# Low parts of split weight chunks: one GpSimd subtraction over eight feature blocks, or four over two

## What is computed

```python
def ab_layer(x, xc, mod, mod_c, w_in, w_out, ...):
    q, k, v, g_a, xb, b_g, c_g, g_b = split_cols(modulate(x, shift, scale) @ w_in, widths)
    ...
    y = jnp.concatenate([o_a * jax.nn.silu(g_a), o_b * jax.nn.silu(g_b)], axis=-1) @ w_out
    x_new = layer_norm(DEEPNORM_ALPHA * x + gate * y, ln_g, ln_b)
    ...
def swiglu(x, w_gate, w_up, w_down):
    return (jax.nn.silu(x @ w_gate) * (x @ w_up)) @ w_down
```

## Time and profile before

| | us |
|---|---|
| median of three runs | 2348.47 |
| lowest, highest | 2347.04, 2351.69 |
| span of the profiled execution | 2345.2 |

### The profile page before, as it was taken

How to read it: one execution, slowest core, us unless ns; L and a number is a source line. 1 busy time by engine, 2 the same in 40 slices (tenths; PEclk the granted TensorE clock), 3 DMA queues, 4 the chain that set the end, 5 groups by cost and what they waited for, 6 DMA issues and landing times. The chain is left out here.

```text
span 2345.2 us, 28077 instructions
## 1 busy us (share of the span) xinstructions
PE 2188.8 (93%) x11735; PEld 1760.2 (75%) x11735; DVE 1079.0 (46%) x1662; ACT 669.4 (29%) x1035; POOL 786.9 (34%) x373
## 2 busy tenths in 40 slices
PE   4999888989999999998898899999998999999998
PEld 3887777866686767886855678888887688888886
DVE  1113664653656565657995543111126684111114
ACT  3223233324545454542112432100113353000111
POOL 1421113401322333325500015553544234554453
PEclk7999999999999999999899999999999999999999
DMA  9232113422111111113111112322322222232322
GB/s 301 70 116 77 55 55 113 123 90 90 36 36 37 36 36 37 36 55 99 41 36 54 55 55 72 103 95 91 108 90 90 82 98 72 90 108 90 94 95 81
DMA packets 174797, 187.47 MB, mean 80 GB/s; under 512 B 25600, under 2 KB 153936, under 8 KB 174544
## 3 DMA queue, kind: packets, MB, share of 16 engines
q1 hardware_dynamic: 164720, 175.42, 24.0%
q10 hardware_dynamic: 9376, 8.16, 1.2%
q0 software_dynamic: 576, 2.10, 0.2%
HBM read 183.56 MB, written 2.10 MB: 79 GB/s over the span
## 5 line engine op out<-in xcount | busy, mean ns | idle before, releaser
L3018 POOL TENSOR_TENSOR weights_lo<-weights_raw,weights_hi 128x2048 fp32r<-128x2048 f32 (+1 forms) x101 | 458.1, 4536 | 858.5 <-ACT weights_hi L1421 662.2
L698 PE MATMUL ring<-input_hi,weights_hi 128*128 128x512 f32 x784 | 305.4, 389 | 4.1 <-POOL weights_lo L3018 4.1
L700 PE MATMUL ring<-input_hi,weights_lo 128*128 128x512 f32 x784 | 305.1, 389 | 0.0
L699 PE MATMUL ring<-input_lo,weights_hi 128*128 128x512 f32 x784 | 305.0, 389 | 0.0
L2845 DVE CAST weights_hi<-weights_raw 128x2048 fp32r<-128x2048 f32 (+1 forms) x72 | 87.6, 1216 | 366.5 <-PE ring L700 174.3
L3006 POOL TENSOR_TENSOR h_w<-h_p 128x512 f32<-128x512 f32 x56 | 72.0, 1286 | 414.9 <-PE ring L1009 310.9
L982 PE MATMUL obank<-acts,weights_raw 128*128 128x512 f32 x384 | 178.5, 619 | 0.0
L698 PEld LDWEIGHTS ring<-input_hi,weights_hi 128*128 128x128 f32 x784 | 147.2, 188 | 36.2 <-issue 5.8
L700 PEld LDWEIGHTS ring<-input_hi,weights_lo 128*128 128x128 f32 x784 | 147.2, 188 | 30.6
L699 PEld LDWEIGHTS ring<-input_lo,weights_hi 128*128 128x128 f32 x784 | 147.2, 188 | 30.4
L991 PE MATMUL obank<-weights_raw,acts 128*128 128x256 f32 x640 | 143.2, 381 | 0.0
(11 more groups left out here) (464 smaller groups left out, 4394.4 us busy)
## 6 DMA issues: line engine op xcount, KB each, us to landing
weights_raw<-in_w_ada SPq DMA_DIRECT2D x24, 1024.0 KB, 5.3
weights_raw<-in_ffn_w_gate SPq DMA_DIRECT2D x22, 1024.0 KB, 5.4
weights_raw<-in_ffn_w_up SPq DMA_DIRECT2D x22, 1024.0 KB, 5.3
weights_raw<-in_w_in_c SPq DMA_DIRECT2D x20, 1024.0 KB, 5.1
weights_raw<-in_ffn_w_down SPq DMA_DIRECT2D x16, 1024.0 KB, 5.0
weights_raw<-in_w_in_ab SPq DMA_DIRECT2D x9, 1024.0 KB, 6.8
weights_raw<-in_ev_w_in SPq DMA_DIRECT2D x8, 1024.0 KB, 5.4
weights_raw<-in_od_w_in SPq DMA_DIRECT2D x8, 1024.0 KB, 5.3
```

The costliest lines, as they stand in the source:

```text
L698: pe.matmul(o, hi[:, k, ms], xh[:, k, t0:t0 + n], start=k == 0, stop=False)
L699: pe.matmul(o, hi[:, k, ms], xl[:, k, t0:t0 + n], start=False, stop=False)
L700: last = pe.matmul(o, lo[:, k, ms], xh[:, k, t0:t0 + n], start=False, stop=k == KD - 1)
L3018: pool.tensor_tensor(W_LO[slot][:, 0:kt, :], WR[:, slot, 0:kt, :], w_hi[:, 0:kt, :], ALU.subtract).then_inc(sem("w_lo"), 1)
```

## The change

The low part of a chunk is made by a loop of subtractions over two feature blocks each (512 elements a partition), four for a chunk of eight blocks and three for one of six. The semaphore goes up with the last one. Nothing else is changed: order, buffers and waits stay.

```diff
                     slot, kt, w_hi = splits[i][:3]
                     pool.wait_ge(*splits[i][6:8])
-                    pool.tensor_tensor(W_LO[slot][:, 0:kt, :], WR[:, slot, 0:kt, :], w_hi[:, 0:kt, :], ALU.subtract).then_inc(sem("w_lo"), 1)
+                    for k0 in range(0, kt, 2):
+                        ks = slice(k0, k0 + 2)
+                        last = pool.tensor_tensor(W_LO[slot][:, ks, :], WR[:, slot, ks, :], w_hi[:, ks, :], ALU.subtract)
+                    last.then_inc(sem("w_lo"), 1)
```

## The result

The changed kernel takes 2355.7 us (median; 2351.77 to 2361.85), the kernel before in the same comparison 2348.47. The ratio is 1.0027, 95% interval 1.0018 to 1.0036: slower by 0.27%, 6.3 us (4.2 to 8.5), where 2354.3 and +5.8 were forecast. (The ratio is not the quotient of the two medians, which lie 7.2 us apart.) The profiled execution spans 2351.3 us, 6.1 more than that of before.

The account below looks back on a forecast made before the run. TensorE, busy 93%, bounds the kernel; GpSimd's low parts count only where TensorE, or something it waits for, stands behind them. Terms 0.7−1.1+0.3+0.7+1.84+0.4−1.2+4.2 = +5.8 on 2348.5 give 2354.3 us, range 2346 to 2361.

Parts of the forecast that it names:

- The price of one chunk: Each GpSimd low part: three more operations cost 0.46 us a chunk, 0.30 for the 1536-element ones; bounds 0.3 to 0.6.
- The steady part of the FFNs costs nothing: 20 FFN chunks: 1.10 us in hand, TensorE needs about 0.25, so 0.85 covers the added 0.46.
- rival 2: An extra operation costs more; from 0.28 us each the 20 FFN chunks lose their cover; at 0.40, 2367 us; chance 0.09.
- Plain waits: Waits at em1.1, fu0.0, rx1 and fu1.0 grow by 0.46 each, +1.84 us, plus +0.4 for hand-overs at rx1.
- First chunk: First products wait for L3024, after the first low part: 0.46 and one hand-over, 0.4 to 1.0, taken +0.7 us.
- 432 us: L2115, shut out, ends about 1.8 us earlier; TensorE's 1.19 wait for the next L2139 caps the gain: taken −1.1.
- 456 to 486 us: Two waits at L884: low part later, TensorE's idle time parted in two; −0.6 if the clock is spared, else +1.6; taken +0.3.
- 1776 us: L2891 let in earlier, ending some 2 us sooner; TensorE's 3.44 wait for n_diag shrinks: −2.0 to −0.5, taken −1.2.
- 1890, rz2: Pieces let in a scan, an L2967 and a scan: 2.1 to 3.2, taken 2.9, plus 1.3 for the clock: +4.2 us.
- 1078 to 1170 us: L2554 freed earlier, c_diag gains 2.0, waited away at L1138; s_w's tables about 1.2 later: −2.0 to +1.7, taken +0.7 us.
- Rival 1: GpSimd keeps the port over its queue; VectorE gains nothing, hand-overs go: +3.7, 2352.2 us; chance 0.12.
- Rival 3: VectorE's early release around 1080 us is kept: −6.4 there instead of +0.7, 2347.2 us; chance 0.19.

Follow-up runs that it names:

- e5: Kernel before with low parts in pieces, except the ten chunks whose low part TensorE waits for, which stay whole; 2349.5 us, ratio 1.0000.
- e9: Kernel before with pieces, each signalled at nine waited-for chunks, one signal elsewhere; q0, y11.0 and y11.1 whole; 2339.75 us, ratio 0.9954.
- e10: Kernel before with nine waited-for chunks in pieces signalled each, y0.3 and rx0 in pieces with one signal, rest whole; 2341.17 us, ratio 0.9959.
- e1: Kernel before, unchanged, run and profiled again; 2349.45 us, ratio 0.9989.
- e3: Kernel before with four pieces only for low parts outside the FFNs' chunks, one operation in the FFNs; 2354.44 us, ratio 1.0008.
- e4: Kernel before with eight pieces of one block for every chunk; 2367.5 us, ratio 1.0077.
- e6: Kernel before with four pieces for every chunk, each piece signalled to TensorE at nine chunks with waits; 2344.65 us, ratio 0.9980.
- e8: Kernel before with two pieces of four blocks for every chunk, one signal at the end; 2349.82 us, ratio 1.0001.
- e2: Kernel before with four pieces only for the 68 chunks of the two FFNs, one operation for the others; 2348.83 us, ratio 0.9993.
- after: The changed kernel: kernel before with every low part in pieces of two blocks and one signal at the end; 2355.7 us, ratio 1.0027.

## Why the prediction was right, and where not

The direction, the mechanism and the list of places held. That +5.8 met +6.3 is in part luck. The places as measured below, with the open one at its forecast of 0.3, add up to 0.53−0.8+0.3+1.8+1.7−1.2+1.98 = +4.3, the lower end of the interval: one large term came out 2.2 too high and another 1.1 too low. In the profile 1.1 more came near 1353 us, where nothing was changed and the granted clock was 0.83 over 20 us instead of 0.91; e5, e9 and e10 have the same there, and e1, e3, e4, e6 and e8 do not. What fills the rest of the median is not shown.

- **The price of one chunk** (0.46): 0.42 in the FFNs. The step was right: linear in the elements, with 0.14 for each extra operation in e4 too (0.98/7). By the estimate from the Trainium skill (GPSIMD Engine Reference, section 3.1) it would have been next to nothing; the trace's 0.42 differs, and decides.
- **The steady part of the FFNs costs nothing:** shown by e2 and by 0.68 us still in hand. Of rival 2's threshold only this can be said: at 0.98 a chunk (e4) the cover is just used up.
- **Plain waits** (4×0.46 + 0.4): 0.44, 0.41, 0.41 and 0.41, 1.7 in all; no turn at rx1, so the 0.4 was not there.
- **First chunk** (+0.7): the wait for L3024 grew from 8.86 to 9.68, and 0.30 came back: +0.53.
- **432 us** (−1.1): the wait at L800 fell from 1.19 to 0.35, −0.8; what TensorE waits for there is now ScalarE's a_probs_t.
- **456 to 486 us** (+0.3): the two waits went from 0.95 and 3.45 to 3.48 and 1.71, the long one moved to the chunk before, and the clock's fall with it. In the profile the stretch from 440 to 500 us is 1.75 shorter, but the unchanged kernel differs by 1.6 there: the term is left open.
- **1776 us** (−1.2): −1.2. The wait for n_diag fell from 3.44 to 2.21 and what was gained stayed.
- **1890, rz2** (+4.2): **mis-sized.** TensorE's wait grew by 1.98, below the lower bound of 2.1 and well below the 2.9 in the sum, and the clock stayed at 1.00. The price of a turn was right: the pieces took 1.40, 1.73, 2.18 and 1.71 us, about 0.4 more than 1.31 beside a short operation and 0.87 more beside the scan. The step that failed is which operations are let in, "a scan, an L2967 and a scan": the low part began while a scan ran, and met an L2967, a scan and an L2967. With those the prediction's own prices give 1.6 to 2.6. The 1.3 for the clock was not there in this execution; a fall cost 1.6 in e3 after a wait of 3.04, and in e8 after 1.95.
- **1078 to 1170 us** (+0.7): **mis-sized, and by another mechanism.** c_diag came 2.3 earlier (2.0 forecast), and all of it went into the wait at L1138, as forecast. But s_w did not come 0.7 later; against the start of that stretch it came about 0.5 earlier. What cost time was the longer wait itself: the clock fell behind it and 2.3 us went there, 1.8 in the sum. e9, with both chunks whole, shows it: no longer wait, no fall, 0.2.

Rival 1 (GpSimd keeps the port) falls with VectorE's rows under the pieces: 1.57 to 2.20 at rz2 instead of 5.50. Ten VectorE operations of over 4 us lay beside low parts of weights before, and none does after. The Trainium skill (SBUF — State Buffer, "Who interferes with whom") says that whoever issues first has the shared port for its whole instruction. The trace agrees: at rz2 the port went over at each end of a piece, to the engine that had been waiting.

Rival 3 falls: nothing of the early release around 1080 us was kept. At L2478 there was next to none. It took 1.26 us instead of 4.58, but the three small operations behind it (L2479 to L2481, 0.17 us each before) then waited for a piece each, 1.21 to 1.22, so that a chain of short operations won 0.2 us in all. Rival 4 falls with the interval of the result.

## What to carry to other kernels

Cutting an operation into pieces helps nobody who waits for the last of them: a consumer that could start on the first must be told of each piece. The same four subtractions made the kernel 0.27% slower with one signal and, with a signal each at the nine chunks that TensorE waits for and three others left whole, 0.46% faster than before. Before giving an engine time back, look at what its consumer waits for next: at c_diag 2.3 us were won, waited away at s_w, and paid once more by the clock.

## What was not expected of the hardware

The clock behind one and the same wait (s_w, L1138) was 1.00 after 0.96, 2.63, 2.69, 3.06 and 3.11 us of idle time, 0.80 and then 0.50 after 3.25, and 0.50 after 4.1 to 5.7. At rz2, where another load went before, it fell after 1.95 (e8) and 3.04 (e3), and not after 3.01 (after). So the length of the wait alone does not tell; in a sum the 1.2 to 2.3 us that a fall cost here belong in the range and not in the term.

The price of a fall may not end with it. Near 1222 us another one (0.86 granted from 1222 to 1234 us in after, 1.7 us lost) stands in six of the seven profiles with a fall behind s_w, and in none of the five without. The profiles of after, e2 and e5 won the 1.7 back near 1283 us; e3, e4 and e6 did not. Whether the first fall brings the second is not shown.

In the first 880 us two executions of one kernel differ by 4 us, more than most of the terms here. Two profiles of it agree within 0.06 us behind that; but with falls that come and go there too, one profile's second part tells a change of 0.2% only place by place, and the median of many runs has to stand beside it.
